# First layer's value product with V as stationary operand; layer norm folded into the router's weights; weight splits reordered

## The reference

```
for i in range(2):
    mix = swa_sink_attention(x, ...) if i == 0 else forgetting_attention(x, ...)
    x = layer_norm(ALPHA * x + mix, ln_gain[i, 0], ln_bias[i, 0])
    ffn = grouped_moe(x, w_router, b_router, w_gate[i], w_up[i], w_down[i])
    x = layer_norm(ALPHA * x + ffn, ln_gain[i, 1], ln_bias[i, 1])
```

## Time and profile before

| | before |
| --- | --- |
| median of 3 runs | 920.74 us (920.06 to 922.89) |
| the profiled execution, its own time | 919.96 us |
| its span | 918.2 us |
| PE busy | 888.0 us (97%) |
| DVE busy | 552.9 us (60%) |
| ACT busy | 392.3 us (43%) |
| mean granted clock of TensorE | 0.996 |

### The profile page before, as it was taken

One profiled execution on the slowest core, in us unless ns is written; L12 is line 12 of the kernel. 1 busy time (PEld: TensorE's weight loads), 2 busy tenths in 40 slices (PEclk: granted clock), 3 DMA queues, 4 the chain that ended last, 5 costly groups with the idle time before them and its releaser, 6 DMA issues.

```text
span 918.2 us, 12501 instructions
## 1 busy us (share of the span) xinstructions
PE 888.0 (97%) x4480; PEld 616.2 (67%) x4480; DVE 552.9 (60%) x1141; ACT 392.3 (43%) x787; POOL 120.1 (13%) x138
## 2 busy tenths in 40 slices
PE   8999999999999999989999999999999999999996
PEld 7887777884666665557878886655786565666553
DVE  4544786548766677773332223777456777677846
ACT  4322787001555655540132224777301355555540
POOL 2000232103010000120000000323111200000030
PEclk9999999999999999999999999999999999999999
DMA  9962000019999998644054222120106999999352
GB/s 347 302 253 92 2 1 1 24 47 351 350 382 389 379 389 322 222 180 163 21 184 138 92 93 92 46 71 24 69 24 241 312 380 382 374 384 406 124 197 96
DMA packets 49446, 182.36 MB, mean 199 GB/s; under 512 B 6496, under 2 KB 6496, under 8 KB 41200
## 3 DMA queue, kind: packets, MB, share of 16 engines
q1 hardware_dynamic: 35712, 132.34, 38.6%
q0 software_dynamic: 9392, 34.12, 11.3%
q10 hardware_dynamic: 4288, 15.21, 4.2%
HBM read 159.60 MB, written 22.05 MB: 198 GB/s over the span
## 4 chain that ended last, share of the span: by engine, by line
PE 89%; DVE 5%; DMA 3%; issue 2%; ACT 1%; SPq 1%; POOL 0%; DVEq 0%; ACTq 0%; POOLq 0%
PE bank L613 17%; PE bank L615 16%; PE bank L614 16%; PE bank L896 11%; PE bank L727 4%; PE bank L708 4%; PE bank L865 3%; PE bank L570 3%; PE bank L752 2%; PE bank L771 2%; PE bank L527 2%; DMA ring<-in_swa_w_in 2%; PE bank L813 2%; PE bank L541 1%; DMA ys<-arena 1%
## 5 line engine op out<-in xcount | busy, mean ns | idle before, releaser
L1492 DVE TENSOR_TENSOR gu_low<-ring,gu_high 128x1024 fp32r<-128x1024 f32 x128 | 151.2, 1221 | 46.9 <-ACT gu_high L1116 46.8
L1116 ACT CAST gu_high<-ring 128x1024 fp32r<-128x1024 f32 x128 | 127.6, 1048 | 18.5 <-DVE arena L1626 18.5
L896 PE MATMUL bank<-ring,arena 128*96 128x512 f32 x256 | 115.8, 595 | 2.0 <-issue 2.0
L613 PE MATMUL bank<-gu_high,rows_high 128*96 128x512 f32 x256 | 113.0, 442 | 2.5 <-DVE rows_low L1610 2.5
L614 PE MATMUL bank<-gu_low,rows_high 128*96 128x512 f32 x256 | 101.5, 397 | 0.0
L615 PE MATMUL bank<-gu_high,rows_low 128*96 128x512 f32 x256 | 101.1, 395 | 0.0
L896 PEld LDWEIGHTS bank<-ring,arena 128*96 128x96 f32 x256 | 39.7, 164 | 55.0 <-issue 54.0
L1048 ACT ACTIVATE arena<-arena,nmax 128x256 f32<-128x256 f32 (+3 forms) x128 | 66.8, 523 | 20.9 <-DVE nmax L1385 10.8
L471 POOL TENSOR_TENSOR low<-ring,high 128x512 fp32r<-128x512 f32 x32 | 40.7, 1272 | 220.5 <-ACT high L1076 220.5
L613 PE MATMUL bank<-high,x_high 128*128 128x512 f32 x160 | 64.2, 401 | 1.3 <-DVE low L1286 1.1
L615 PE MATMUL bank<-high,xlow 128*128 128x512 f32 x160 | 62.9, 393 | 0.0
(11 more groups left out here) (244 smaller groups left out, 1543.7 us busy)
## 6 DMA issues: line engine op xcount, KB each, us to landing
ring<-in_w_gate SPq DMA_DIRECT2D x32, 1024.0 KB, 12.3
ring<-in_w_up SPq DMA_DIRECT2D x32, 1024.0 KB, 15.0
ring<-in_w_down SPq DMA_DIRECT2D x32, 1024.0 KB, 14.9
ring<-in_fox_w_in SPq DMA_DIRECT2D x6, 2048.0 KB, 9.4
ys<-arena ACTq DMA_DIRECT2D x28, 384.0 KB, 7.7
ys<-lnp POOLq DMA_DIRECT2D x1, 4608.0 KB, 24.3
ring<-in_swa_w_in SPq DMA_DIRECT2D x2, 2048.0 KB, 17.2
ring<-in_swa_w_o SPq DMA_DIRECT2D x2, 2048.0 KB, 15.9
```

What stands on the lines that cost most here:

```text
L613: eng.matmul(out, ah, wh, start=(c == 0), stop=False)
L896: mm = eng.matmul(bank[5 + half][0:CAP, :], hT[:, b, c, :], w[:, c, half * BLK:(half + 1) * BLK], start=(c == 0), stop=(c == FC - 1))
L1116: eng.copy(gu_high[u % 2][:, :, part, :], slot_gate_up(use)[:, :, part, :]).then_inc(S("gu_high"), 1)
L1492: eng.tensor_tensor(gu_low[use % RING][:, :, part, :], slot_gate_up(use)[:, :, part, :], gu_high[u % 2][:, :, part, :], ALU.subtract).then ...
```

## The change

1. **First layer's attention.** `mix`, `turn_out` and `normalise` are gone; the first layer goes through `mix_cols`, `sums`, `spread_sums`, `take_shares` and `divide` as the second does. `sums` gains the addition of the sink's exponential; it stands on DVE behind `evac_probs` of a pair's last step and ahead of the masks.
2. **Router.** `turn_x` transposes the state with the residual added but before the norm. The router's weights are made once for each layer: multiplied by the norm's gain, with their column mean taken off; the product of the norm's bias with the router's weights goes into `bl`. The logits are then (raw state x weights) times `rstd`, plus `bl`. To make them: four small DMAs on SP's queue, on PE one transpose and eight matmuls on 64 columns behind groups 8 and 9 of the input projection, 11 small DVE operations. In the W_o stage `turned_norm(t)` first copies the transposed tile out and then centres and scales; for tiles 0 to 2 it stands in the next tile's turn. ACT copies the transposed tile out before it issues the tile's store. The hum behind `route(2)` is 4 long and not 16. On DVE one more small operation works on the logits.
3. **Order.** The low parts of the first expert's weights are made two by two behind tiles 1 and 2. Of the eight splits of the value weights between the layers, two stay and six go behind tile 1's first statistics and tile 0's low part. `open_banks` stands ahead of the last transposes of the expert stage, and one semaphore serves both. Tile 1's input and the rotary table share a semaphore.

```
-        wr = sb("wr", [P, KC, NE])
+        wr = sb("wr", [P, DEPTH, KC, NE])
...
+                        for i in range(2 * DEPTH):
+                            vec = (ln_gain, ln_bias)[i % 2][i // 2, 0]
+                            eng.dma_start(ln_rows[KC * i:KC * i + KC, :], vec.rearrange("(c p) -> c p", p=P)).then_inc(S("const_in"), 16)
...
+                elif a in ("00", "10"):
+                    eng.wait_ge(S("res_done"), 2 * (t + 1) + OUT_BLOCKS * NT * int(a[0]))
...
+                            if k == GROUPS[0] - 4:
+                                eng.wait_ge(S("const_in"), 144)
+                                eng.transpose(bank[7][:, 0:4 * KC], ln_rows[0:4 * KC, :], ident[0:4 * KC, 0:4 * KC]).then_inc(S("wr_pe"), 1)
+                            if k == GROUPS[0] - 3:
+                                eng.wait_ge(S("consts"), 1)
+                                eng.wait_ge(S("wr_dve"), 1)
+                                for c in range(KC):
+                                    mm = eng.matmul(bank[7][:, 0:4 * NE], ones, wr_ln[:, c, :, :].rearrange("p j n -> p (j n)"),
...
                     for i in range(k1 - k0):
                         for half in range(2):
...
-                            v = HD * (2 * hp + half)
+                            v = HD * (2 * hp // (NH // NKV) if l == 0 else 2 * hp + half)
                             mm = eng.matmul(bank[5 + hp % 2][HD * half:HD * half + HD, n * P:(n + 1) * P],
-                                            V[:, k0 + i, v:v + HD], pT[:, half, i * P:(i + 1) * P],
+                                            (V0 if l == 0 else V)[:, k0 + i, v:v + HD], pT[:, half, i * P:(i + 1) * P],
...
-                        (mix if l == 0 else mix_cols)(s - 1)
+                        mix_cols(s - 1)
...
-                    if l == 0 and s >= NT and s % NT == 1:
-                        turn_out(s // NT - 1)
...
-                hum(16)
+                hum(4)
...
-                    if l == 1 and s % NT == NT - 1:
+                    if s % NT == NT - 1:
                         sums(s // NT)
...
-                        (normalise if l == 0 else divide)(s // NT - 1)
+                        divide(s // NT - 1)
...
+                def turned_norm(t):
+                    v = xres[:, t, :]
+                    evac_x_tile(f"{l}0", t)
...
+                    link(eng.scalar_tensor_tensor(v, v, mv[:, t, 0:1], lnp[:, 0, :], ALU.subtract, ALU.mult))
+                    eng.wait_ge(S(f"rstd{l}0"), t + 1)
+                    eng.scalar_tensor_tensor(v, v, rstd[:, t:t + 1], lnp[:, 1, :], ALU.mult, ALU.add).then_inc(S(f"x_ready{l}0"), 1)
...
-                link(eng.tensor_tensor(lg, lps, tiles(br[:, :]), ALU.add))
+                link(eng.tensor_tensor(lg, lps, over(rstd[:, :], NE), ALU.mult))
+                link(eng.tensor_tensor(lg, lg, tiles(bl[:, l, :]), ALU.add))
...
-                    value_weights_low(KC, 2 * KC)
+                    value_weights_low(KC, KC + 2)
...
+                                if t == 1:
+                                    value_weights_low(KC + 2, 2 * KC)
```

More of the change, by code:

```diff
@@ L723, in turn_probs @@
                             eng.wait_ge(S(f"pT_ready{half}"), STEPS * l + s)
-                        if l == 1 and s > NT and s % NT == 1:
-                            eng.wait_ge(S(f"shares_here{half}"), s // NT)
+                        if s > NT and s % NT == 1:
+                            eng.wait_ge(S(f"shares_here{half}"), PAIRS * l + s // NT)
                         for i in range(k1 - k0):
@@ L936, in _ @@
                 eng.wait_ge(S("placed"), 2 * l + 2)
+                open_banks(l, 0)
                 for h in range(2):
@@ L1417, in take_shares, with sums @@
                     eng.tensor_copy(shares[:, hp % 2, 3 * P:4 * P], bank[4][:, P:2 * P]).then_inc(S("shares_here1"), 1)
-                def normalise(hp):
+                def sums(hp):
                     eng.wait_ge(S("exp_done"), 2 * STEPS * l + 2 * NT * (hp + 1))
+                    if hp >= 2:
+                        eng.wait_ge(S("aT_ready"), PAIRS * l + hp - 1)
                     rs = rsum[:, hp % 2, :, :]
```

157 lines of the change are left out of this document (68 added, 89 removed).

## The result

| | before | changed |
| --- | --- | --- |
| median of 4 runs each | 920.45 us (920.06 to 922.89) | 928.32 us (926.8 to 929.16) |
| ratio, 95% interval | | 1.0081 (1.0065 to 1.0096) |
| the profiled execution | 919.96 us | 926.8 us |
| its span | 918.2 us | 925.0 us |
| mean granted clock | 0.996 | 0.990 |

The change costs 7.5 to 8 us. The forecast was 921.3 with a range of 915.5 to 925.5, so both missed. The page of the changed kernel (its first part) already says that the time isn't work: PE is busy for the same 888.0 us as before, in a span 6.8 us longer.

A forecast was written before the change was run, and what follows sets the result against it. PE was taken as the bound, DVE and ACT close. Terms +2.0 + 2.0 - 1.0 - 0.8 - 1.6 = +0.6 took the profiled 919.96 to 920.6, as a median 921.3 us; 8 in 10 range 915.5 to 925.5.

The forecast's parts named there:

- Making the router's weights: Behind groups of the input projection: eight products and a transpose on PE add +2.0 us, bounds 1.7 to 4.0.
- The attention pairs: First layer's attention: a pair of heads takes 8.65 us instead of 8.36, seven pairs +2.0 us, bounds -4.6 and +5.9.
- The last step: From a pair's last step to the next pair's first: PE waits for the reciprocals' spread, 2.7 us instead of 1.85.
- The second step is copy, masks, sinks' shift: 2.0: Second step of a pair in the first layer's attention, costed by DVE's operations: 2.0 us, 2.2 before.
- The end of attention: From the last transposes to W_o's first matmul: 3.2 us instead of 4.26, -1.0 us.
- The router's path: Behind the last W_o group: row numbers 2.0 us early, but the gather waits for the store; together -0.8 us.
- Between the layers: PE's idle 1.60 us before the second layer goes, as tile 0's statistics start sooner: -1.6 us, bounds -1.8 and 0.
- The clock: Rival, chance 0.10: PE idles more between hum and gather, the first layer may also lose clock; 1.7 us lost, kernel 923.0.
- The long pair: Rival, chance 0.14: first layer's pairs take about 9.2 us, costing +5.9 instead of +2.0; kernel 925.2 us.
- The pair follows DVE's load: Rival, chance 0.12: first layer's pairs take 7.7 us, giving -4.6 instead of +2.0; kernel 914.7 us.

The follow-up runs named there:

- vectors_late: The changed kernel with GpSimd's loads of the next norm's gain and bias issued behind the first four gathers; 920.36 us, ratio 1.0003 to the kernel before.
- att_alone: The kernel before with only the new form of the first layer's attention; 925.17 us, ratio 1.0056 to the kernel before.
- pool_zeros: The changed kernel with GpSimd writing zeros for the low parts of the first layer's W_o weights instead of subtracting; 926.3 us.
- simple: The kernel before with the next norm's loads behind the first four gathers and the value weights' splits divided into two and six; 917.03 us, ratio 0.9965.

## Why the prediction was wrong

- **Making the router's weights**, +2.0 taken, 2.5 found from start to first scores, 2.14 of it in the rows of the transpose and the products (0.24 and 1.90). Right.
- **The attention pairs**, +2.0 taken for 8.65 us a pair, +5.5 found for 9.15. This is the step that failed, in two of its terms, and it is 3.5 of the 6.2 us between the 920.6 forecast for the profiled execution and its 926.8; the clock is 1.6, the router's path 0.7. The last step was right (2.7 taken, 2.75 found). "The second step is copy, masks, sinks' shift: 2.0" went by DVE's load with the shift at its old 0.66; it took 2.61, as the shift met the start of GpSimd's split. Net of what the third step took back that is 0.22 a pair, 1.5 us in seven. The other 0.28 a pair, 2.0 us, remain with the meeting gone: the steps of 2.0, 2.0 and 1.95 took 2.09, 2.04 and 2.06. They were costed engine by engine, from the reading that PE is the bound because it is busy for 7.94 of 8.36 us. The rows show in its place a loop through exponential, transposes, product and copy, which takes 2.03; this part is read from the trace, not tested by a run.
- **The end of attention**, -1.0 taken; 3.48 instead of 4.26, so -0.8. Right.
- **The router's path**, -0.8 taken, -0.1 found. The store was issued 1.7 us later and took 9.5, and the gather left on it, 0.8 us earlier in the first layer (0.2 forecast) and 1.5 in the second (0.6 forecast). What failed is the silent step after it, that a gather lands a fixed time behind its issue: its flight grew by 0.8 and 1.4 us, and vectors_late, with 1 MB less ahead of it, took 0.5 and 1.4 of that back.
- **Between the layers**, -1.6 taken, -1.9 found. Right.
- **The clock** was a rival at 0.10, priced 1.7 us, and came true in the first layer by its own condition, in addition to the other losses. It should have been weighed together with the router term, since the same 2 us of earliness that were to be the gain stretched PE's idling. The count above would have put it far over 0.10 once the hums end 1.5 us ahead of the rows.
- **The rivals.** The long pair was priced right (9.2, and 925.17 us in att_alone) for a wrong reason: no engine was full. In 9.15 us PE is busy for 7.96, DVE for 7.96 with 1.07 of waiting in it, ACT for 7.33. "The pair follows DVE's load" is refuted by pool_zeros: with DVE relieved of 1.1 us of waiting the pair lost 0.23.

The sum of the found terms, 2.5 + 4.6 + 0.0 + 1.6 - 1.9, is the 6.8 us of the spans; the small rows of the table come to about zero.

## What to carry to other kernels

An operation that took 0.66 us on eight numbers a partition was waiting here. Compare such an operation with its like (0.16), and find its partner before moving anything, because each move changed the wait. Eight products that got 0.35 us shorter on PE were worth nothing in a step that is a loop through ACT, so trace one full round of the loop before adding up loads. And row numbers that were ready 1.6 us earlier gained nothing until bulk loads that nobody needed yet were taken out of the way of the gather; in simple, where the row numbers came last, taking them away gained nothing either.

## What was not expected of the hardware

- A DVE operation on two SBUF operands waits for the end of a GpSimd subtraction in flight: 0.16 us of work took 1.23, 1.25 and 0.32 us, 0.69 took 1.77. The wait is not shown as idle time: the record of the operation is longer. A GpSimd memset of 0.53 us did not hold it (0.17), and DVE's operations with a PSUM input were never held in the first layer's attention (masks 0.48, copies 0.42).
- 1 MB of loads that start 0.3 us behind a store, on another queue, cost the rows of the changed kernel 1.4 and 1.8 us in its two layers; in simple, where the gather waits for the row numbers, they cost nothing.
- Executions of the kernel before, on the chips of these runs, took from 917.1 to 925.6 us, with a mean clock of 0.997 for the shortest and 0.989 for the longest. By an estimate from these two, 0.008 of 920 us, 7 of the 8.4 us are clock. A stretch of 3.3 us at half clock is 1.65 us, so a difference of 0.3% between two kernels can be one such stretch in each layer.
